# A second mixer's scan: weight subtractions on GpSimd, keys ahead of queries, interleaving copies ahead of weight copies

## The chip, the cores and the metric

One core of one Trainium2 chip runs the whole program in one launch. The metric is the device time of one execution in microseconds. The kernel before takes 1975.9 us (median of three runs, 1975.22 to 1977.95). All arithmetic is 32-bit. Engines are called by the names of the profile: PE (TensorE), PEld (its weight loads), DVE (VectorE), ACT (ScalarE), POOL (GpSimd), SP (SyncE, which issues most DMAs).

## The reference

Two layers. Each has a half-step SwiGLU FFN, a token mixer, and a second half-step FFN, for 256 latent tokens and 256 context tokens. The mixer projects its input, runs a gated linear recurrence in both directions for four heads, and in parallel a pooling mixer:

```python
proj = u @ w_in
q, zf, zb, i, g, pv, ga, gb = jnp.split(proj, IN_SPLITS, axis=-1)
o, s_f, s_b = hgrn2_bidir(q, i, zf, zb, lb_f, lb_b, s0_f, s0_b)
if not need_out:
    return None, s_f, s_b
on = o * lax.rsqrt(jnp.mean(o * o, axis=-1, keepdims=True) + EPS)
a = (on.reshape(...) * hg_norm_w * jax.nn.silu(g))
p = pool_mixer(pv, pool_w, pool_scale, on_grid)
merged = jax.nn.sigmoid(ga) * (a @ w_a) + jax.nn.sigmoid(gb) * (p @ w_b)
return merged @ w_out, s_f, s_b
```

The recurrence is S_t = diag(f_t) S_{t-1} + k_t v_t^T, o_t = S_t^T q_t. In the second (last) layer the context tokens yield only their final states: queries are needed for 256 tokens, keys and gates still for 512. So the first mixer works on 512 tokens, the second on 256 for all but keys, gates and values.

## The kernel before, in words

**Weights in two parts.** Weights arrive in units of 128 x 1024 numbers, in a ring of four slots. For each unit SP issues a DMA into `raw` as soon as the slot's last unit is multiplied (`s_used`); ACT copies it to `w_hi` in the rounded format (`split_next`, L712, signal `s_hi`); DVE writes the rest, raw minus `w_hi`, to `w_lo`, which lies in the memory of `raw` (`split_lo`, L980, signal `s_lo`); PE multiplies w_hi by u_hi, w_hi by u_lo, and w_lo by u_hi (L333, L334, L335). Both splits run three units (`AHEAD`) ahead of PE.

**The scan.** Each head's 256-token recurrence is a tree of doubling blocks in ten steps. Step 0 is the diagonal; steps 1 to 7 join blocks of 1, 2, ... 64 tokens; step 8 joins the two 128-token halves; step 9 applies the context's final states. Array `S` (two buffers, one for even and one for odd heads) has four parts: part 0 forward keys, 1 and 2 queries, 3 backward keys; `T` has the gates' products over blocks. For step k:

- DVE updates the keys and queries with the gates (`carry` in `prepare_step`, L1186): two instructions in the first mixer, four in the second (parts 0, 1, 2, 3 in this order). The last one signals `s_prep`.
- ACT interleaves the directions into `mixed` by two copies, keys first, queries second (`mix_directions`, L825), signal `s_mix`. This is done for steps 1 to 7.
- PE multiplies keys by queries (L496), signal `s_score`.
- DVE merges the scores into `A` under a mask (`merge`, L1232) and doubles the gate products (`double_totals`, L1207).

**Order.** Nothing schedules: each engine runs its own list in the order in which the code writes it, and waits at semaphores. A head is 12 pieces. In each piece PE does half a weight unit of projections for the next head (in the last head: of the gate and pooling projections) and then one scan step. In piece p, DVE waits for mixing copy p, prepares step p+1, in odd pieces subtracts the weight unit (`lo_next`), then merges step p and doubles. In piece p, ACT first copies the weight unit (odd pieces), then interleaves step p+1, then does the projections' activations. Small parts of the head before stand between: `head_diag`, `head_gate` and `head_lo` on DVE (L1215, L1220) and `head_hi` on ACT (L837).

**After the scan** of a mixer ACT and DVE copy the pooling projection to `pv` (L899, L1297), PE multiplies it by box matrices (L633), which POOL's DMAs (`mixer_tables`, L312) have brought to memory that the scan used. POOL does only DMA issues and a few memsets.

Of the kernel before, what the change touches and what calls it, by code (L numbers as in the profile page):

```python
# [29 lines left out]
F32 = mybir.dt.float32  # L30
# [8 lines left out]
ALL = 2 * TOK  # L39
# [4 lines left out]
NH = 4  # L44
# [57 lines left out]
def program(nc, resid_in, c_in, c_cols_in, cols_in, poolw_in, box_in, masks_in, ident_in, weights, adaw, out):  # L102
    with ExitStack() as stack:
# [118 lines left out]
        s_vout = sem("v_out")  # L222
        s_sga = sem("sig_a_out")
        s_prep = sem("operands_ready")
        s_mix = sem("directions_mixed")
# [64 lines left out]
        def _(pool):  # L290
# [27 lines left out]
            load(ahead, N_ADA - ahead)  # L318
            mixer_tables(1)

# [383 lines left out]
        def _(act):  # L704
# [112 lines left out]
            def mix_directions(n, step, nt):  # L817


                act.wait_ge(s_prep, NSTEP * n + step + 1)  # L820

                act.wait_ge(s_score, NSTEP * n + step - 1)
                hb = 1 << (step - 1)
                for m, (array, other) in enumerate(((0, 3), (1, 2))):
                    ins = act.activation(view(mixed, (step % 2 * 2 + m) * ALL, [2 * hb, nt // (2 * hb)], [hb, 2], [1, hb]),  # L825
                                         view(S[n % 2], array * ALL, [2 * hb, nt // (2 * hb)],
                                              [(other - array) * ALL + hb, 2], [1, hb]), ACT.Copy)
                ins.then_inc(s_mix, 1)
# [10 lines left out]
            def mixer(layer, n_norm):  # L839
# [18 lines left out]
                for head in range(NH):  # L858
                    n = layer * NH + head
                    par = head % 2  # L860
                    for piece in range(12):
                        j = piece // 2
                        if piece % 2:
                            split_next(base + j - (base + j) % 4, None, (base + j) % 4 + AHEAD)
                        if piece < NLEVEL:
                            mix_directions(n, piece + 1, nt)
                        if piece % 2:
# [100 lines left out]
        def _(dve):  # L968
# [200 lines left out]
            def prepare_step(n, step):  # L1169
# [21 lines left out]
                else:  # L1191
                    carry(0, 1, 0, ALL, 0)
                    carry(1, 1, 0, nt, 1)

                if nt == ALL:
                    ins = carry(2, 2, 1, ALL, 0)
                else:
                    carry(2, 1, 1, nt, 0)
                    ins = carry(3, 1, 1, ALL, 1)
                ins.then_inc(s_prep, 1)  # L1200
# [34 lines left out]
            def mixer(layer, n_norm):  # L1235
# [14 lines left out]
                for head in range(NH):  # L1250
                    n = n0 + head
                    par = head % 2
                    for piece in range(12):
                        j = piece // 2
                        lo_next = lambda: split_lo(base + j - (base + j) % 4, None, (base + j) % 4 + AHEAD)
                        if piece < NSTEP:
# [36 lines left out]
                    base += 6  # L1293

                dve.wait_ge(s_used, base)
                for t in range(nt // P // 2, nt // P):
# [229 lines left out]
```

## Time and profile before

| | |
|---|---|
| median of three runs | 1975.9 us |
| the profiled execution | 1976.28 us, span 1974.6 us |
| PE busy | 1942.9 us (98%) |
| DVE busy | 1262.6 us (64%) |
| ACT busy | 795.4 us (40%) |
| POOL busy | 72.7 us (4%) |
| granted TensorE clock | 0.997 of full speed |

The span runs from the first to the last instruction that the profiler sees; the execution's own time is 1.7 us more. The scan of the first mixer lies at about 459 to 643 us of the span, that of the second at about 1560 to 1688 us. Idle time is shown in front of an instruction with the engine whose work ended it.

### The profile page before, as it was taken

The page shows a single profiled execution, that of the slowest core. Times are in us where ns is not written, and L with a number is a line of the kernel's source. Part 1 is how long each engine was busy: PE and PEld are TensorE (multiplying, and loading weights), DVE is VectorE, ACT ScalarE, POOL GpSimd, SP SyncE. Part 2 cuts the span into 40 slices and gives each one's busy share as a digit, 9 for nine tenths or more (in the row PEclk, how much of TensorE's full clock was granted, in tenths as well). Part 3 has the DMA queues.
Part 4 walks back from the last instruction along what each step waited for, and adds up shares of the span by engine and source line. Part 5 has one row for each costly group of instructions (what it writes and reads, how often), then busy time and mean ns, then how long its engine had stood idle before and what let it go on. Part 6 is the DMA issues. An engine that isn't in the chain of part 4 may idle for free.

```text
span 1974.6 us, 29022 instructions
## 1 busy us (share of the span) xinstructions
PE 1942.9 (98%) x10024; PEld 1649.4 (84%) x10024; DVE 1262.6 (64%) x2048; ACT 795.4 (40%) x1083; POOL 72.7 (4%) x142
## 2 busy tenths in 40 slices
PE   7999999999999999999999999999999998999998
PEld 2888888888888888888888888888888897999998
DVE  3667576676665466667566675755757678575555
ACT  2422222345554323532222353223224576456444
POOL 0000000000000000000000000000100000000000
PEclk9999999999999999999999999999999999999999
DMA  7345445433223243345454534444544333545554
GB/s 311 107 150 190 139 162 177 158 105 111 71 69 112 87 139 121 111 139 202 138 160 168 161 96 151 169 160 141 205 140 129 99 105 105 178 149 182 183 184 154
DMA packets 78664, 287.39 MB, mean 146 GB/s; under 512 B 8768, under 2 KB 10048, under 8 KB 77824
## 3 DMA queue, kind: packets, MB, share of 16 engines
q1 hardware_dynamic: 58912, 212.89, 32.5%
q0 software_dynamic: 19392, 73.34, 11.4%
q8 instruction: 46, 0.75, 0.2%
q14 instruction: 26, 0.21, 0.0%
q10 hardware_dynamic: 288, 0.18, 0.0%
HBM read 285.34 MB, written 1.05 MB: 145 GB/s over the span
## 4 chain that ended last, share of the span: by engine, by line
PE 92%; DVE 3%; DMA 2%; issue 1%; ACT 1%; ACTq 0%; DVEq 0%; SPq 0%
PE bank L333 26%; PE bank L334 26%; PE bank L335 26%; DMA raw<-weights 2%; PE bank L689 1%; PE bank L496 1%; PE bank L556 1%; PE bank L550 1%; PE bank L551 1%; ACT w_hi L712 1%; DVE S L1186 1%; PE bank L633 1%; PE bank L361 1%; PE bank L417 1%; PE bank L411 0%
## 5 line engine op out<-in xcount | busy, mean ns | idle before, releaser
L333 PE MATMUL bank<-u_hi,w_hi 128*128 128x512 f32 (+1 forms) x1824 | 664.0, 364 | 0.4 <-DVE w_lo L980 0.4
L334 PE MATMUL bank<-u_lo,w_hi 128*128 128x512 f32 (+1 forms) x1824 | 654.7, 359 | 0.0
L335 PE MATMUL bank<-u_hi,w_lo 128*128 128x512 f32 (+1 forms) x1824 | 654.6, 359 | 0.0
L980 DVE TENSOR_TENSOR w_lo<-raw,w_hi 128x1024 fp32r<-128x1024 f32 x384 | 469.1, 1223 | 245.8 <-ACT w_hi L712 216.5
L712 ACT ACTIVATE w_hi<-raw 128x1024 fp32r<-128x1024 f32 x384 | 405.1, 1056 | 435.1 <-DMA raw<-weights 434.4
L333 PEld LDWEIGHTS bank<-u_hi,w_hi 128*128 128x128 f32 x1824 | 344.5, 189 | 51.5 <-DVE w_lo L980 1.0
L335 PEld LDWEIGHTS bank<-u_hi,w_lo 128*128 128x128 f32 x1824 | 344.3, 189 | 51.3
L334 PEld LDWEIGHTS bank<-u_lo,w_hi 128*128 128x128 f32 x1824 | 344.6, 189 | 50.3 <-issue 0.7
L333 PE MATMUL bank<-hid_hi,w_hi 128*128 128x512 f32 (+1 forms) x832 | 299.1, 360 | 0.7 <-DVE w_lo L980 0.5
L991 DVE SCALAR_TENSOR_TENSOR junk<-ada_raw,silu_c 128x1024 bf16<-128x1024 f32 x256 | 298.2, 1220 | 0.5 <-DVE junk L991 0.5
L335 PE MATMUL bank<-hid_hi,w_lo 128*128 128x512 f32 (+1 forms) x832 | 298.2, 358 | 0.0
L334 PE MATMUL bank<-hid_lo,w_hi 128*128 128x512 f32 (+1 forms) x832 | 298.2, 358 | 0.0
L778 ACT ACTIVATE silu_t<-bank 128x512 f32<-128x512 f32 (+1 forms) x88 | 47.9, 545 | 355.9 <-PE bank L335 353.5
L1107 DVE TENSOR_TENSOR hid_t<-silu_t,bank 128x512 f32<-128x512 f32 (+1 forms) x88 | 54.7, 621 | 206.3 <-ACT silu_t L778 205.9
L333 PEld LDWEIGHTS bank<-hid_hi,w_hi 128*128 128x128 f32 x832 | 157.1, 189 | 24.8 <-DVE w_lo L980 0.7
L335 PEld LDWEIGHTS bank<-hid_hi,w_lo 128*128 128x128 f32 x832 | 157.1, 189 | 23.2
L334 PEld LDWEIGHTS bank<-hid_lo,w_hi 128*128 128x128 f32 x832 | 157.2, 189 | 23.1 <-issue 0.2
L1082 DVE SCALAR_TENSOR_TENSOR h<-bank,gate_c,h 128x256 f32 (+1 forms) x192 | 85.3, 479 | 74.5 <-PE bank L335 72.0
L305 POOL DMA_DIRECT2D ada_raw<-adaw x126 | 66.8, 530 | 1209.1 <-DVE junk L991 1209.1
L1111 DVE TENSOR_TENSOR hid_lo<-hid_t,hid_hi 128x512 f32 (+1 forms) x88 | 55.1, 626 | 77.8 <-ACT hid_hi L780 77.8
L1186 DVE TENSOR_TENSOR S<-S,T 128x256 f32<-128x256 f32 (+1 forms) x192 | 78.7, 465 | 19.7 <-PE bank L487 11.6
L780 ACT ACTIVATE hid_hi<-hid_t 128x512 f32 (+1 forms) x88 | 51.0, 580 | 71.0 <-DVE hid_t L1107 71.0
(162 smaller groups left out, 1504.5 us busy)
## 6 DMA issues: line engine op xcount, KB each, us to landing
raw<-weights SPq DMA_DIRECT2D x384, 512.0 KB, 3.5
ada_raw<-adaw POOLq DMA_DIRECT2D x128, 512.0 KB, 4.3
start_w<-weights SPq DMA_DIRECT2D x8, 1024.0 KB, 12.5
box<-box POOLq DMA_DIRECT2D x4, 1024.0 KB, 8.0
h<-resid SPq DMA_DIRECT2D x1, 2048.0 KB, 19.5
silu_c<-c POOLq DMA_DIRECT2D x1, 1024.0 KB, 5.2
out<-sig_a SPq DMA_DIRECT2D x8, 128.0 KB, 2.0
poolw<-poolw POOLq DMA_DIRECT2D x2, 256.0 KB, 10.0
```

Of the source, the lines that this page charges most:

```text
L305: pool.dma_start(ada_raw[:, j, :], adaw[bass.ds(i * 2 + j, 1)].rearrange("a p n -> (a p) n")).then_inc(s_aland[j], 16)
L333: pe.matmul(ps, w_hi[:, slot, k, :], hi(k), start=first, stop=False)
L334: pe.matmul(ps, w_hi[:, slot, k, :], lo(k), start=False, stop=False)
L335: mm = pe.matmul(ps, w_lo[:, slot, k, :], hi(k), start=False, stop=last)
L712: act.activation(view(w_hi, (j % RING) * UNIT, [1, UNIT]), raw[:, j % RING, :], ACT.Copy).then_inc(s_hi, 1)
L780: act.activation(hid_hi[:, bass.ds(i * 2 + b, 1), 0:nt].rearrange("p a n -> p (a n)"), hid_t[:, b, 0:nt], ACT.Copy).then_inc(s_hid_hi, 1)
L980: dve.tensor_tensor(view(w_lo, (j % RING) * UNIT, [1, UNIT]), raw[:, j % RING, :], view(w_hi, (j % RING) * UNIT, [1, UNIT]).bitcast(F32), ...
L991: dve.scalar_tensor_tensor(out=junk[:, s, :], in0=ada_raw[:, j, :], scalar=1.0, in1=silu_c[:, s, :], op0=ALU.mult, op1=ALU.mult, accum_out ...
L1082: ins = dve.scalar_tensor_tensor(out=hd, in0=ps[:, span(s)], scalar=gate_c[:, s, bass.ds(d, 1)], in1=hd, op0=ALU.mult, op1=ALU.add)
L1107: dve.tensor_tensor(hid_t[:, b, 0:nt], silu_t[:, b, 0:nt], bank[2 * b + 1][:, 0:nt], ALU.mult).then_inc(s_up_free, 1)
L1111: dve.tensor_tensor(hid_lo[:, bass.ds(f, 1), 0:nt].rearrange("p a n -> p (a n)"), hid_t[:, b, 0:nt], hid_hi[:, bass.ds(f, 1), 0:nt].rearra ...
L1186: return dve.tensor_tensor(t, t, view(Th, d * ALL + (1 - side) * hb, *cut, [0, hb]), ALU.mult)
```

## The change

Three edits:

1. On ACT, in both mixers, the interleaving copies of a piece stand ahead of its weight copy.
2. In the second mixer, for steps 2 and up, DVE updates parts 3 and 0 (both keys) first and signals `s_keys`; the first interleaving copy waits for that alone, the second for `s_prep`.
3. The 24 weight subtractions of the second mixer's scan move from DVE to POOL. They stand behind all loads of the modulation weights; POOL's three table DMAs stand between the 22nd and the 23rd. DVE waits for the last of them before its `pv` copy.

```diff
             load(ahead, N_ADA - ahead)
-            mixer_tables(1)
+
+            scan_unit = mix_base(1) + 8 + AHEAD
+            pool.wait_ge(s_lo, scan_unit - START)
+            for u in range(scan_unit, scan_unit + 6 * NH):
+                if u == scan_unit + 6 * NH - 2:
+                    mixer_tables(1)
+                pool.wait_ge(s_hi, u + 1 - START)
+                pool.tensor_tensor(view(w_lo, u % RING * UNIT, [1, UNIT]), raw[:, u % RING, :],
+                                   view(w_hi, u % RING * UNIT, [1, UNIT]).bitcast(F32), ALU.subtract
+                                   ).then_inc(s_lo, 1)
...
             def mix_directions(n, step, nt):
-                act.wait_ge(s_prep, NSTEP * n + step + 1)
-
                 act.wait_ge(s_score, NSTEP * n + step - 1)
+                if nt < ALL and step > 1:
+                    act.wait_ge(s_keys, (NSTEP - 2) * (n - NH) + step - 1)
                 hb = 1 << (step - 1)
                 for m, (array, other) in enumerate(((0, 3), (1, 2))):
+                    if m or nt == ALL or step == 1:
+                        act.wait_ge(s_prep, NSTEP * n + step + 1)
...
+                        if piece < NLEVEL:
+                            mix_directions(n, piece + 1, nt)
                         if piece % 2:
                             split_next(base + j - (base + j) % 4, None, (base + j) % 4 + AHEAD)
-                        if piece < NLEVEL:
-                            mix_directions(n, piece + 1, nt)
...
                 else:
                     carry(0, 1, 0, ALL, 0)
-                    carry(1, 1, 0, nt, 1)
+                    carry(3, 1, 1, ALL, 1).then_inc(s_keys, 1)
...
                 else:
-                    carry(2, 1, 1, nt, 0)
-                    ins = carry(3, 1, 1, ALL, 1)
+                    carry(1, 1, 0, nt, 1)
+                    ins = carry(2, 1, 1, nt, 0)
                 ins.then_inc(s_prep, 1)
...
-                        lo_next = lambda: split_lo(base + j - (base + j) % 4, None, (base + j) % 4 + AHEAD)
+                        lo_next = lambda: None if layer else split_lo(
+                            base + j - (base + j) % 4, None, (base + j) % 4 + AHEAD)
...
+                if layer:
+                    dve.wait_ge(s_lo, base + AHEAD - START)
                 dve.wait_ge(s_used, base)
```

ACT, first mixer, second head, pieces 0 to 3, before (L825 interleaving copies, x2 is one step; L712 weight copy; L837 a part of the head before; the others are activations of projections):

```order
L832 ACTIVATE r_cols<-bank,eps_c 128x4
L825 ACTIVATE mixed<-S_67 128x512 x2
L712 ACTIVATE w_hi<-raw 128x1024
L825 ACTIVATE mixed<-S_67 128x512 x2
L809 ACT_TABLE_LOAD
L809 ACTIVATE S_63<-bank 128x512
L825 ACTIVATE mixed<-S_67 128x512 x2
L837 ACTIVATE hid_hi<-head_t 128x512
L712 ACTIVATE w_hi<-raw 128x1024
L825 ACTIVATE mixed<-S_67 128x512 x2
L813 ACT_TABLE_LOAD
```

The same place of the changed kernel (L837 is now the interleaving copy, L722 the weight copy, L849 the part of the head before):

```order
L844 ACTIVATE r_cols<-bank,eps_c 128x4
L837 ACTIVATE mixed<-S_67 128x512 x4
L722 ACTIVATE w_hi<-raw 128x1024
L819 ACT_TABLE_LOAD
L819 ACTIVATE S_63<-bank 128x512
L837 ACTIVATE mixed<-S_67 128x512 x2
L849 ACTIVATE hid_hi<-head_t 128x512
L837 ACTIVATE mixed<-S_67 128x512 x2
L722 ACTIVATE w_hi<-raw 128x1024
L823 ACT_TABLE_LOAD
```

Each weight copy of an odd piece has moved behind the interleaving copies of that piece. DVE's list in the first mixer has not moved: its subtraction still stands between the carries and the merge.

DVE, second mixer, third head, pieces 2 and 3, before (L1186 carries, in parts 0, 1, 2, 3; L980 subtraction; L1232 merge; L1207 doubling):

```order
L1232 COPY_PREDICATED A_65<-masks,bank 128x2x128
L1207 TENSOR_TENSOR T_64<-T_64 128x256
L1215 TENSOR_TENSOR head_t<-head_t,bank 128x256
L1186 TENSOR_TENSOR S_63<-S_63,T_64 128x64x4
L1186 TENSOR_TENSOR S_63<-S_63,T_64 128x32x4 x2
L1186 TENSOR_TENSOR S_63<-S_63,T_64 128x64x4
L980 TENSOR_TENSOR w_lo<-raw,w_hi 128x1024
L1232 COPY_PREDICATED A_65<-masks,bank 128x2x128
L1207 TENSOR_TENSOR T_64<-T_64 128x128
L1220 TENSOR_TENSOR hid_lo<-head_t,hid_hi 128x256
```

The same pieces of the same head in the changed kernel:

```order
L1244 COPY_PREDICATED A_65<-masks,bank 128x2x128
L1219 TENSOR_TENSOR T_64<-T_64 128x256
L1227 TENSOR_TENSOR head_t<-head_t,bank 128x256
L1198 TENSOR_TENSOR S_63<-S_63,T_64 128x64x4 x2
L1198 TENSOR_TENSOR S_63<-S_63,T_64 128x32x4 x2
L1244 COPY_PREDICATED A_65<-masks,bank 128x2x128
L1219 TENSOR_TENSOR T_64<-T_64 128x128
L1232 TENSOR_TENSOR hid_lo<-head_t,hid_hi 128x256
```

The subtraction is gone from DVE's list, and the two keys' carries (the longer shape, 512 tokens) stand ahead of the two queries' carries.

POOL, end of its list, changed kernel (L306 the last loads of modulation weights, L327 subtractions, L313 and L314 the tables' DMAs):

```order
L306 DMA ada_raw<-adaw 128x1024
L302 REGISTER_ALU
L302 COMPARE_AND_BRANCH
L327 ISA
L327 TENSOR_TENSOR w_lo<-raw,w_hi 128x1024 x22
L313 DMA box_60<-box 128x2048
L313 DMA box_61<-box 128x2048
L314 DMA poolw<-poolw 128x512
L327 TENSOR_TENSOR w_lo<-raw,w_hi 128x1024 x2
```

Before, the tables' DMAs came directly behind the loads; now 22 subtractions stand ahead of them and two behind.

## Rows read from the trace of the kernel before

**Rows 1.** The page: span, then busy time of each engine.
```profile
span 1974.6 us, 29022 instructions
PE 1942.9 (98%) x10024; PEld 1649.4 (84%) x10024; DVE 1262.6 (64%) x2048; ACT 795.4 (40%) x1083; POOL 72.7 (4%) x142
```

**Rows 2.** The page's chain of waits, shares of the span by engine.
```profile
PE 92%; DVE 3%; DMA 2%; issue 1%; ACT 1%; ACTq 0%; DVEq 0%; SPq 0%
```

**Rows 3.** Waits of PE, first mixer's scan (440 to 640 us); us, times, longest.
```profile
PE bank L496 <- ACT mixed L825: 0.5, 1, 0.5
```

**Rows 4.** Waits of PE, second mixer's scan (1500 to 1695 us).
```profile
PE bank L496 <- ACT mixed L825: 5.8, 5, 1.8
PE bank L478 <- DVE S L1186: 2.0, 2, 1.3
PE bank L633 <- DVE pv L1297: 1.1, 1, 1.1
```

**Rows 5.** Timeline, PE, first mixer: start, us, instruction, [idle before].
```profile
464.22 1.13 PE L496 MATMUL bank<-mixed 128*128 128x128 f32 x8 [0.53 <-ACT mixed L825]
471.56 1.05 PE L496 MATMUL bank<-mixed 128*128 128x128 f32 x8
...
522.16 1.05 PE L496 MATMUL bank<-mixed 128*128 128x128 f32 x8
525.78 1.05 PE L496 MATMUL bank<-mixed 128*128 128x128 f32 x8
```

**Rows 6.** Timeline, ACT, first mixer.
```profile
462.45 1.63 ACT L825 ACTIVATE mixed<-S 128x512 f32<-128x512 f32 x2 [3.81 <-DVE S L1176]
...
518.52 1.04 ACT L712 ACTIVATE w_hi<-raw 128x1024 fp32r<-128x1024 f32 x1
519.47 1.14 ACT L825 ACTIVATE mixed<-S 128x512 f32<-128x512 f32 x2
...
523.73 1.16 ACT L825 ACTIVATE mixed<-S 128x512 f32<-128x512 f32 x2 [0.72 <-DVE S L1186]
```

**Rows 7.** Timeline, DVE, first mixer, second head.
```profile
517.87 1.28 DVE L1186 TENSOR_TENSOR S<-S,T 128x512 f32<-128x512 f32 x2
519.60 1.23 DVE L980 TENSOR_TENSOR w_lo<-raw,w_hi 128x1024 fp32r<-128x1024 f32 x1 [0.44 <-ACT w_hi L712]
520.74 0.73 DVE L1232 COPY_PREDICATED A<-masks,bank 128x512 f32<-128x512 uint8 x1
521.36 0.41 DVE L1207 TENSOR_TENSOR T<-T 128x128 f32<-128x128 f32 x1
521.80 0.69 DVE L1220 TENSOR_TENSOR hid_lo<-head_t,hid_hi 128x512 fp32r<-128x512 f32 x1
```

**Rows 8.** Timeline, PE, second mixer.
```profile
1585.80 0.70 PE L478 MATMUL bank<-S 128*128 128x256 f32 x2 [0.72 <-DVE S L1186]
...
1665.27 0.68 PE L496 MATMUL bank<-mixed 128*128 128x128 f32 x4 [1.16 <-ACT mixed L825]
...
1671.47 0.68 PE L496 MATMUL bank<-mixed 128*128 128x128 f32 x4 [1.55 <-ACT mixed L825]
```

**Rows 9.** Groups of instructions, DVE, 1500 to 1695 us, shapes apart.
```profile
L980 DVE TENSOR_TENSOR w_lo<-raw,w_hi 128x1024 fp32r<-128x1024 f32 x38 | 46.4, 1223 | 36.5 <-ACT w_hi L712 28.0 <-PE bank L480 8.3
L1207 DVE TENSOR_TENSOR T<-T 128x512 f32<-128x512 f32 x4 | 2.7, 686 | 0.0
```

**Rows 10.** Groups of instructions, POOL, whole span, shapes apart.
```profile
L291 POOL MEMSET ones<- 128x128 f32 x1 | 0.2, 205 | 0.3 <-POOLq L1517 0.3
L292 POOL MEMSET eps_c<- 128x1 f32 x1 | 0.1, 99 | 0.0
```

**Rows 11.** Timeline, all engines, end of the second mixer's scan.
```profile
1677.32 1.05 POOL L312 DMA_DIRECT2D box<-box  x2 [183.90 <-PE bank L496]
...
1687.78 1.06 ACT L712 ACTIVATE w_hi<-raw 128x1024 fp32r<-128x1024 f32 x1 [1.95 <-DMA raw<-weights]
...
1691.24 1.10 PE L633 MATMUL bank<-box,pv 128*128 128x256 f32 x4 [1.14 <-DVE pv L1297]
```

More of the change, by code:

```diff
@@ L223, in program @@
         s_sga = sem("sig_a_out")
+        s_keys = sem("keys_ready")
         s_prep = sem("operands_ready")
```

## The prediction

> **What bounds the kernel now.** I read the page's totals first, then the chain of waits, then PE's waits in each mixer's scan, then the timelines of the places where something waits. PE is busy 98% of the span [rows 1] and makes 92% of the chain that ended last [rows 2]. So time can be won only where PE stands idle, and it is lost wherever some other engine becomes late for PE. In the first mixer's scan PE waits once for an interleaving copy, 0.5 us [rows 3]: nothing is to be won there. In the second it waits five times for interleaving copies, 5.8 us, twice for carries, 2.0 us, and once for the copy to pv, 1.1 us [rows 4]. There PE's work per piece is shorter (256 tokens), while DVE's is not: DVE ends last. The largest possible gain is therefore about 9 us, 0.45% of the time.
>
> **Edit 1 in the first mixer: the weight copy goes behind the interleaving copies.** ACT has room, but DVE is in order, and in this mixer it still subtracts the weight unit between its carries and its merge. Before, the weight copy ran during the carries, and DVE found it done or nearly done (idle 0.44 us in [rows 7]). Now the weight copy begins only when the interleaving copies end, and these begin only when the carries end. So DVE stands still for 1.15 + 1.05 us after the carries of every odd piece.
>
> Second head, from [rows 6, 7]. Carries start at 517.87 and end at 519.15 (unchanged, since they depend on PE's scores). Interleaving copies, 1.15: 520.35. Weight copy, 1.05: 521.4. Subtraction, 1.14 from its start to that of the merge: 522.6. Merge, 0.62: 523.2. Doubling and the part of the head before, 0.44 + 0.61: 524.25. Carries of step 5, 1.28: 525.55. Interleaving, 1.15: 526.7. PE starts about 0.15 later, at 526.85. Before, this copy ended at 523.73 + 1.16 = 524.89, and PE took it at 525.78 [rows 5]: 0.9 us of slack against 1.8 us of delay. PE waits 1.1 us.
>
> From there the chain closes on itself, from one odd step to the next: carries 1.28, interleaving 1.15, weight copy 1.05, subtraction 1.14, merge 0.62, doubling 0.3 (0.41 in [rows 7], and less in each step after), carries 1.28, interleaving 1.15, signals 0.2, together 8.2 us. PE's two pieces take 2 x 3.62 = 7.25 us [rows 5]. Step 7 waits another 0.9 us. So 2.0 us for the second head, and for the third, which repeats it. In the first head nothing of an earlier head stands between: from the end of the first copies (462.45 + 1.63 = 464.08, [rows 6]) the same chain with a longer doubling (0.69 for 512 wide, [rows 9]) ends at 472.7, PE wants it at 471.56 [rows 5]: 1.2 us, then 0.9 twice, 3.0 us. In the fourth head a projection's activation already delays PE a little; I take 1.7 us. Sum 8.7 us lost, in a scan that waited 0.5 us before. Bounds: 0 if the copies overlap in a way that I don't see, 11 us if every one of the twelve pairs costs 0.9.
>
> **Edits 1 and 2 in the second mixer.** Interleaving no longer stands behind a weight copy that itself waits for its DMA, and the keys' copy runs under the queries' carries, so one step's loop shortens by some 0.4 us. The 1.8 us wait of the first step [rows 4] stays: ahead of that step stands the subtraction of the unit before the moved ones, which is still DVE's. With DVE free of the subtractions the four other waits for copies (5.8 - 1.8 = 4.0 us, two of them in [rows 8]) and the two for carries (2.0 us) can go; ACT's table loads in the last head leave some 0.5. That is -5.5 us, if POOL's work costs DVE nothing.
>
> **Edit 3: the price of POOL's subtraction.** The trace has no two-input instruction on POOL. Its 128-wide memset takes 205 ns and its 1-wide one 99 ns [rows 10], so 0.83 ns per element and pass, 0.85 us for 1024. From below, DVE's own 1.22 us [rows 9]; from above, two reads and a write one after the other, 2.65 us. I take two passes, 1.8 us. For PE alone either is hidden: units are prepared three ahead, over 10 us.
>
> What is not hidden is DVE. The trace shows no moment in which POOL computes beside DVE, so its effect is bounded by two cases: none, or the two engines take turns at the memory for each instruction in which DVE reads two operands from it. These are the carries and doublings, which make up most of the chain. If they take turns, each subtraction that starts holds up the next doubling for 1.8 us, where before it took 1.14 us of DVE's time. At the 0.72 us wait in [rows 8] DVE's run was subtraction, merge, doubling, carries. The merge reads its scores from PSUM and may run beside the hold (0.3 us, half of the 0.62 for twice the tokens), so the run ends 1.8 - 1.14 - 0.3 = 0.4 us later, and where the hold of the odd piece before has pushed on this one as well, 1.0 us. That gives +1.0, +1.1, +0.4 us for three heads. In the fourth the shorter loop and the longer hold cancel. So +2.5 us instead of -5.5; up to +8 if the hold is 2.65 us and breaks in between the carries. I take turn-taking as the likelier: it is my choice, and no row decides it.
>
> The Trainium skill bears on this. "SBUF — State Buffer", section "Who interferes with whom", says that a VectorE instruction with two SBUF inputs contends with a GpSimd one that reads SBUF, and that the later one is blocked until the first ends. No run here shows it yet. "GPSIMD Engine Reference", section "Performance versus the Vector engine", has 4497 ns for a 2048-wide fp32 add against 2293 ns on VectorE; half of it, an estimate, is 2.2 us, and by that the sum would be some 2 us more. DVE's 1.22 us in this trace agrees with half of the page's VectorE figure.
>
> **The end of the scan.** POOL's list now has 22 subtractions ahead of the tables' DMAs. Before, they were issued at 1677.32 as soon as step 7 was scored; now the subtraction of that piece comes first, some 1.8 us. Behind, the last of the 24 weight units waited for its DMA until 1687.78, in competition with these tables; it is then subtracted, DVE copies pv, and PE starts at 1691.24 after 1.14 us idle [rows 11]. Now: later tables end later and hold the weight unit some 0.7 us longer; POOL's subtraction takes 0.7 us more than DVE's; and DVE's copy waits for it. +1.4 us (0.3 to 3).
>
> **The sum.** Against the profiled execution, 1976.28 us: +8.7 + 2.5 + 1.4 = +12.6, 1988.9 us. The median of the runs shown lies 0.4 lower: 1988.5 us.
>
> **Rivals.**
> - *POOL computes beside DVE freely.* +8.7 - 5.5 + 1.4 = +4.6, 1980.5 us. For it: nothing in the trace, as nothing against it.
> - *The first mixer absorbs the new order, engines take turns.* 0 + 2.5 + 1.4: 1979.8 us. For it: PE waits 0.5 us in that whole scan [rows 3]. Against: the slack before step 5 is 0.9 us and I count 1.8.
> - *Faster: the first mixer absorbs the order and POOL runs freely.* The second mixer's loop becomes shorter than PE's piece, its waits vanish: -5.5 + 1.4 = -4.1, 1971.8 us. It decides once DVE's delay per odd piece in the first mixer is under 0.9 us and a doubling beside a POOL subtraction keeps its length.
>
> **Chances.** Forecast 0.5; free POOL 0.25; first mixer absorbs, turns 0.15; faster 0.1. What a measurement of this kernel tells from no change is 0.2%, 4 us. The forecast and nearly all of the second case are slower; the third is about half within; of the last, two thirds faster. Faster 0.08, same 0.17, slower 0.75. Range 1976 to 1994: it leaves out the fastest case and holds of more than 2.65 us.
>
> **What would show it.** In the first mixer: DVE's subtraction idle some 2 us before it, behind the weight copy, in odd pieces; PE waiting for L496 two or three times a head, 7 to 10 us in all. If PE's waits there stay under 2 us, the first step is wrong. In the second: doublings or carries of two or more us beside a POOL subtraction, and PE waits of 8 to 13 us against 7.8; if doublings keep 0.2 to 0.7 us and the waits fall to 2 us, the free case holds. At the end: PE's idle before the first box product at 2 to 3 us instead of 1.14.

## The result and the profile after

The changed kernel takes 2006.9 us (median of four runs, 2002.81 to 2011.03) against 1976.9 us for the kernel before on the same chip: ratio 1.0151, interval 1.0138 to 1.0164. It is slower, as forecast, but by 30 us where 12.6 were forecast, and outside the range. Its profiled execution took 2002.81 us. Ratios compare a kernel with the kernel before on the same chip, whose median was 1976.2 us beside e1 to e4, 1978.4 beside e5 to e8 and 1977.6 beside e9 to e12. Executions of one kernel differ in their granted clock: the other three of the changed kernel took 4 to 8 us longer than the profiled one, at a mean of 0.990 to 0.991 against 0.993, and one of the ten of e6 took 3397.5 us at 0.649 and is left out of its ratio.

The page of the changed kernel: span and busy time, to be held against [rows 1].

```profile
span 2001.1 us, 29026 instructions
PE 1951.4 (98%) x10024; PEld 1654.2 (83%) x10024; DVE 1272.2 (64%) x2024; ACT 796.0 (40%) x1083; POOL 131.0 (7%) x166
```

Two things don't fit. DVE lost 24 instructions of 1.22 us, 29 us of work, and is 10 us busier. And PE is 8.5 us busier with the same 10024 matmuls. The first is a cost on DVE that the instruction list doesn't show; the second must be matmuls that took longer, at a slower clock or otherwise.

Below are the waits of PE in the first mixer's scan (440 to 660 us), and below them in the second's (1500 to 1725 us); us in total, times, longest. They answer to [rows 3, 4]. PE never waits for POOL's result itself in these scans: every wait is for a copy of ACT or a result of DVE.

```profile
PE bank L506 <- ACT mixed L837: 7.1, 9, 1.2
PE bank L560 <- ACT sig_a L888: 0.9, 1, 0.9
...
PE bank L506 <- ACT mixed L837: 9.0, 8, 2.3
PE bank L497 <- DVE S L1198: 5.6, 3, 2.2
PE bank L643 <- DVE pv L1312: 2.9, 1, 2.9
PE bank L488 <- DVE S L1198: 2.8, 1, 2.8
```

**First mixer.** The timeline of DVE in the second head answers to [rows 7]. The idle time before the subtraction was 0.44 us and is 2.2, behind ACT's weight copy (L722), which stands behind the interleaving copies.

```profile
521.22 1.29 DVE L1198 TENSOR_TENSOR S<-S,T 128x512 f32<-128x512 f32 x2
524.74 1.23 DVE L992 TENSOR_TENSOR w_lo<-raw,w_hi 128x1024 fp32r<-128x1024 f32 x1 [2.23 <-ACT w_hi L722]
525.88 0.73 DVE L1244 COPY_PREDICATED A<-masks,bank 128x512 f32<-128x512 uint8 x1
```

**Second mixer.** First POOL, then DVE, in the same stretch of the timeline.

```profile
1588.53 2.52 POOL L327 TENSOR_TENSOR w_lo<-raw,w_hi 128x1024 fp32r<-128x1024 f32 x1 [3.35 <-ACT w_hi L722]
1592.68 2.48 POOL L327 TENSOR_TENSOR w_lo<-raw,w_hi 128x1024 fp32r<-128x1024 f32 x1 [1.63 <-ACT w_hi L722]
1595.81 2.38 POOL L327 TENSOR_TENSOR w_lo<-raw,w_hi 128x1024 fp32r<-128x1024 f32 x1 [0.65 <-ACT w_hi L722]
```

```profile
1588.73 2.47 DVE L1198 TENSOR_TENSOR S<-S,T 128x128 f32<-128x128 f32 x1
1591.13 0.43 DVE L1244 COPY_PREDICATED A<-masks,bank 128x256 f32<-128x256 uint8 x1
1591.46 0.18 DVE L1219 TENSOR_TENSOR T<-T 128x16 f32<-128x16 f32 x1
1591.74 1.16 DVE L1198 TENSOR_TENSOR S<-S,T 128x256 f32<-128x256 f32 x4
1592.83 0.45 DVE L1244 COPY_PREDICATED A<-masks,bank 128x256 f32<-128x256 uint8 x1
1593.16 2.04 DVE L1219 TENSOR_TENSOR T<-T 128x8 f32<-128x8 f32 x1
1595.23 3.31 DVE L1198 TENSOR_TENSOR S<-S,T 128x256 f32<-128x256 f32 x4
```

Read the ends together. POOL's subtraction of 1588.53 ends at 1591.05, and the small carry that came 0.2 us after it ends at 1591.20: 2.47 us for one that took 0.29 before. The doubling at 1593.16 writes 8 columns and takes 2.04 us; it ends at 1595.20, POOL's subtraction of 1592.68 at 1595.16. The run of four carries takes 1.16 us nearly alone and 3.31 with a subtraction in its midst. The merge at 1592.83, whose scores come from PSUM, runs inside a subtraction and keeps its 0.45 us. PE waits 2.80 us for those carries, until 1598.59. In the whole scan 19 of POOL's 24 subtractions catch an instruction of DVE in this way: 13 carries, three doublings and three products of the first step (L1187). Each of them takes 1.75 to 2.58 us and ends 0.03 to 0.28 us after POOL's.

Groups of DVE, shapes apart (busy, mean ns | idle before): the carries before (1500 to 1695 us), then carries and merges of the changed kernel and POOL's group (1500 to 1725 us). The merges took 443 ns before.

```profile
L1186 DVE TENSOR_TENSOR S<-S,T 128x256 f32<-128x256 f32 x64 | 27.0, 422 | 4.1 <-ACT mixed L825 3.4
L1186 DVE TENSOR_TENSOR S<-S,T 128x128 f32<-128x128 f32 x64 | 15.6, 286 | 0.0
```

```profile
L1198 DVE TENSOR_TENSOR S<-S,T 128x128 f32<-128x128 f32 x64 | 39.6, 659 | 0.0
L1198 DVE TENSOR_TENSOR S<-S,T 128x256 f32<-128x256 f32 x64 | 28.6, 488 | 3.7 <-PE bank L497 1.5 <-ACT mixed L837 1.4
L1244 DVE COPY_PREDICATED A<-masks,bank 128x256 f32<-128x256 uint8 x28 | 12.4, 442 | 1.8 <-PE bank L506 1.5
...
L327 POOL TENSOR_TENSOR w_lo<-raw,w_hi 128x1024 fp32r<-128x1024 f32 x24 | 58.7, 2446 | 151.7 <-ACT w_hi L722 151.7
```

**The clock.** Windows of 2 us at the end of the scan: after busy times (PE, PEld, DVE, ACT, POOL) stand the granted clock (1.00 is 2.4 GHz, 0.50 is 1.2), the DMA share and GB/s. The row behind them is PE's box products there, and the last one the same products before.

```profile
1712.00:1714.00 2.00, 0.56 (x5) 0.35 (x3) 0.00 (x0) 1.97 (x4) 1.73 (x1) 1.00 0.31 74
1714.00:1716.00 2.00, 0.51 (x2) 0.49 (x3) 1.31 (x4) 1.98 (x3) 0.62 (x1) 1.00 0.67 238
1716.00:1718.00 2.00, 2.00 (x8) 1.59 (x7) 1.14 (x2) 1.99 (x4) 0.00 (x0) 0.64 0.01 4
1718.00:1720.00 2.00, 2.00 (x6) 1.64 (x5) 1.10 (x1) 0.56 (x3) 0.00 (x0) 0.50 0.00 0
```

```profile
1715.49 5.38 PE L643 MATMUL bank<-box,pv 128*128 128x256 f32 x16 [2.94 <-DVE pv L1312]
```

```profile
1691.24 3.69 PE L633 MATMUL bank<-box,pv 128*128 128x256 f32 x16 [1.14 <-DVE pv L1297]
```

After 2.94 us without work PE soon runs at half its clock, and the 16 box products take 5.38 us where the same 16 took 3.69. That comes on top of the wait. Two more such stretches lie in this stage, behind waits of 2.23 us (until 1630.9) and 2.28 us (until 1692.2). But not every wait of this length is followed by one. Behind the longest wait for carries, 2.80 us, the clock stays at 1.00, and so it does behind one of 2.24 us (until 1666.6):

```profile
1598.59 0.70 PE L488 MATMUL bank<-S 128*128 128x256 f32 x2 [2.80 <-DVE S L1198]
```

```profile
1600.00:1602.00 2.00, 2.00 (x16) 1.95 (x15) 1.37 (x4) 0.60 (x1) 0.00 (x0) 1.00 0.00 0
```

**The account.** Two stages are taken between the three places where DVE prepares a norm (`diag`): ahead of the first mixer (411.5 us before, 411.3 after), ahead of the second, and ahead of the last FFN. So differences elsewhere fall out. The first time in each row is the norm ahead of the second mixer, in the next row that ahead of the last FFN. Kernel before, then changed kernel:

```profile
L1023 DVE TENSOR_TENSOR diag<-ident,r_cols x2: 424/425/426, 1518.2 to 1518.8; 128x256 f32<-128x256 f32 x2
L1023 DVE TENSOR_TENSOR diag<-ident,r_cols x2: 424/424/425, 1768.8 to 1967.1; 128x256 f32<-128x256 f32 x2
```

```profile
L1035 DVE TENSOR_TENSOR diag<-ident,r_cols x2: 425/426/426, 1527.4 to 1528.0; 128x256 f32<-128x256 f32 x2
L1035 DVE TENSOR_TENSOR diag<-ident,r_cols x2: 424/424/424, 1794.7 to 1993.6; 128x256 f32<-128x256 f32 x2
```

The stage with the first mixer is 9.4 us longer (1116.1 against 1106.7), that with the second 16.7 us (267.3 against 250.6), the rest 0.4: together the 26.5 us between the spans. Below is the same reading of e1 to e10, as differences from before, each from one profiled execution. PE's waits are those of the second mixer's scan up to the box products (8.9 us before); "clock" is the time that the lowered clock takes from the second stage, summed over windows of 2 us as (1 - granted clock) x 2:

| kernel | first stage | second stage | PE's waits, second scan | clock |
|---|---|---|---|---|
| changed kernel | +9.4 | +16.7 | +11.4 | 5.1 |
| e1, first mixer's order back | +0.1 | +15.9 | +10.8 | 5.1 |
| e2, order alone | +8.1 | +17.9 | +10.7 | 6.8 |
| e3, POOL alone | +0.1 | +17.8 | +10.6 | 6.8 |
| e4, keys alone | 0.0 | -0.5 | -1.8 | 1.7 |
| e5, POOL subtracts for nobody | 0.0 | +46.0 | +33.9 | 10.3 |
| e6, POOL fills for nobody | 0.0 | -1.2 | -1.0 | 0 |
| e7, subtraction in quarters | +9.4 | +4.5 | +3.2 | 0 |
| e8, DVE subtracts late | +0.1 | +3.7 | +0.5 | 3.4 |
| e9, the same, old order | 0.0 | -0.1 | -1.8 | 1.9 |
| e10, quarters, first mixer's order back | 0.0 | +6.3 | +3.6 | 1.7 |

Waits and clock make up the second stage in every row to within about 2 us.

### The profile page after: what moved, and what is told of

The parts are those of the page before. It is cut to its first block, busy times and chain, and to the rows that moved or that the text cites. A ratio compares the mean times of both kernels' runs of the same rounds, so it can differ in the third digit from the quotient of the medians.

```text
span 2001.1 us, 29026 instructions
## 1 busy us (share of the span) xinstructions
PE 1951.4 (98%) x10024; PEld 1654.2 (83%) x10024; DVE 1272.2 (64%) x2024; ACT 796.0 (40%) x1083; POOL 131.0 (7%) x166
## 4 chain that ended last, share of the span: by engine, by line
PE 89%; DVE 5%; issue 2%; ACT 2%; DMA 1%; POOLq 0%; POOL 0%; ACTq 0%; DVEq 0%; SPq 0%
PE bank L343 25%; PE bank L344 25%; PE bank L345 25%; DVE S L1198 2%; PE bank L699 1%; ACT mixed L837 1%; PE bank L506 1%; PE bank L560 1%; PE bank L561 1%; PE bank L566 1%; DMA raw<-weights 1%; ACT w_hi L722 1%; DVE T L1219 1%; PE bank L371 1%; PE bank L643 1%
## 5 line engine op out<-in xcount | busy, mean ns | idle before, releaser
L992 DVE TENSOR_TENSOR w_lo<-raw,w_hi 128x1024 fp32r<-128x1024 f32 x360 | 439.6, 1222 | 248.7 <-ACT w_hi L722 227.8
L722 ACT ACTIVATE w_hi<-raw 128x1024 fp32r<-128x1024 f32 x384 | 404.6, 1055 | 429.6 <-DMA raw<-weights 428.6
L306 POOL DMA_DIRECT2D ada_raw<-adaw x126 | 66.5, 528 | 1210.6 <-DVE junk L1003 1210.6
L1198 DVE TENSOR_TENSOR S<-S,T 128x256 f32<-128x256 f32 (+1 forms) x192 | 106.9, 612 | 18.3 <-PE bank L497 8.8
L837 ACT ACTIVATE mixed<-S 128x512 f32<-128x512 f32 (+1 forms) x112 | 57.4, 551 | 74.4 <-DVE S L1198 57.0
```

The lines of the kernel that those rows point to most:

```text
L306: pool.dma_start(ada_raw[:, j, :], adaw[bass.ds(i * 2 + j, 1)].rearrange("a p n -> (a p) n")).then_inc(s_aland[j], 16)
L722: act.activation(view(w_hi, (j % RING) * UNIT, [1, UNIT]), raw[:, j % RING, :], ACT.Copy).then_inc(s_hi, 1)
L992: dve.tensor_tensor(view(w_lo, (j % RING) * UNIT, [1, UNIT]), raw[:, j % RING, :], view(w_hi, (j % RING) * UNIT, [1, UNIT]).bitcast(F32), ...
L1198: return dve.tensor_tensor(t, t, view(Th, d * ALL + (1 - side) * hb, *cut, [0, hb]), ALU.mult)
```

## The experiments

The theory after the result: POOL and DVE take turns, for the whole of an instruction, wherever both read two operands from SBUF; the order costs the first mixer what was forecast; the rest is clock. The rivals: POOL's result comes too late for PE; any work of POOL slows DVE; the clock fell for another reason.

**e1: the old order back in the first mixer.**

```diff
+                        if piece % 2 and not layer:
+                            split_next(...)
                         if piece < NLEVEL:
                             mix_directions(n, piece + 1, nt)
-                        if piece % 2:
+                        if piece % 2 and layer:
                             split_next(...)
```

> The changed kernel with ACT's old order in the first mixer only (weight copy ahead of the interleaving copies). Theory: the new order costs the first mixer its 17 or so waits of DVE for the weight copy and through them PE's 8.0 us of waits (7.1 for interleaving copies and 0.9 for a projection's activation); they go back to 0.7 us, and nothing else moves: 2006.9 - 7.5 = 1999 us (1996 to 2002). Rival (what the first mixer loses would be lost later anyway, at the next point where PE waits): 2004 to 2007 us.

Measured: 1993.75 us, ratio 1.0097 (1.0079 to 1.0115). The first stage is back (+0.1), PE waits there 0.6 + 0.2 us, and the second stays at +15.9. So edit 1 costs the first mixer 9.3 us, and the two mixers' losses add up. The time lies below the expected 1996 to 2002 us: the two profiled spans differ by 9.9 us, the medians by 13, and no trace shows the rest.

**e2: edit 1 alone**, in both mixers, on the kernel before.

```diff
-                        if piece % 2:
-                            split_next(...)
                         if piece < NLEVEL:
                             mix_directions(n, piece + 1, nt)
+                        if piece % 2:
+                            split_next(...)
```

> The kernel before with edit 1 alone: interleaving copies ahead of weight copies in both mixers, DVE subtracts everywhere. Theory (a subtraction in DVE's list must not stand behind a weight copy that stands behind copies that need DVE's own carries): first mixer +7.5 us as in the changed kernel; second mixer a chain of 1.2 + 0.7 + 1.05 + 1.14 + 0.33 + 0.3 + 1.2 + 0.7 + 0.2 = 6.8 us for two pieces of which PE needs 3.75 (256 tokens) or 6.4 us (512): +8 to +15 us there, and some us of lower clock: 1993 to 2006 us. Rival (in the second mixer the copies won't wait behind the weights' DMAs any more, so that this edit alone gains there): 1976 + 7.5 - 4 = 1980 us.

Measured: 2002.33 us, ratio 1.0131 (1.0116 to 1.0145). The first mixer loses 8.1 us. The second loses 17.9, though POOL does nothing: the same mechanism as in the first, for DVE still subtracts here. Timeline of DVE there, and PE's waits in that scan (5.8 us before):

```profile
1626.42 1.23 DVE L980 TENSOR_TENSOR w_lo<-raw,w_hi 128x1024 fp32r<-128x1024 f32 x1 [1.74 <-ACT w_hi L712]
1627.57 0.43 DVE L1232 COPY_PREDICATED A<-masks,bank 128x256 f32<-128x256 uint8 x1
```

```profile
PE bank L496 <- ACT mixed L825: 18.2, 10, 3.1
```

**e3: edit 3 alone** (POOL's subtractions; ACT and the carries as before).

```diff
+                pool.wait_ge(s_hi, u + 1 - START)
+                pool.tensor_tensor(view(w_lo, ...), raw[:, u % RING, :], view(w_hi, ...), ALU.subtract).then_inc(s_lo, 1)
...
-                        lo_next = lambda: split_lo(...)
+                        lo_next = lambda: None if layer else split_lo(...)
```

> The kernel before with edit 3 alone: the 24 subtractions on GpSimd, everything else as before. Theory (each GpSimd subtraction blocks VectorE's two-operand instructions for its 2.4 us): carries or doublings of 2 to 3 us beside each, PE's waits in the second mixer's scan about 20 us against 8.9, first mixer unchanged, some us of lower clock: 1987 to 1997 us. Rival (the engines work side by side and only the later copy to pv costs): 1976 - 5 + 3 = 1974 us.

Measured: 1997.13 us, ratio 1.0114 (1.0092 to 1.0136), at the upper edge of what was expected. First stage +0.1, second +17.8. With 24 instructions of 1.22 us taken off DVE, PE waits 10.6 us longer (19.5 us, about 20 expected).

**e4: edit 2 alone** (keys ahead of queries).

```diff
-                    carry(1, 1, 0, nt, 1)
+                    carry(3, 1, 1, ALL, 1).then_inc(s_keys, 1)
...
-                    carry(2, 1, 1, nt, 0)
-                    ins = carry(3, 1, 1, ALL, 1)
+                    carry(1, 1, 0, nt, 1)
+                    ins = carry(2, 1, 1, nt, 0)
```

> The kernel before with edit 2 alone: keys' carries first with their own signal, the first interleaving copy waits for that alone. Theory: the copies end some 0.35 us earlier in each step of the second mixer where ACT is free; PE's waits there fall from 8.9 to 6 to 8 us: 1974 to 1976.5 us, at most 0.1% faster. Rival (the copies wait for the weight copy and its DMA, not for the carries): the same time as before within 0.5 us.

Measured: 1977.47 us, ratio 1.0005 (0.9995 to 1.0015): no change, and not the gain of up to 0.1% that was expected. PE's waits fall from 8.9 to 7.1 us, as expected, but this profile has one low stretch of the clock (1568 to 1573 us) that the profile before has not.

**e5: the kernel before, with POOL subtracting for nobody.** DVE keeps its own subtractions.

```diff
+                pool.wait_ge(s_hi, u + 1 - START)
+                pool.tensor_tensor(ada_raw[:, 1, :], ada_raw[:, 0, :], silu_c[:, 0, :], ALU.subtract).then_inc(s_side, 1)
```

> The kernel before, DVE subtracting as there, with 24 GpSimd subtractions added in the second mixer's scan whose operands (the table ada_raw and silu_c) and result nobody uses, each released by the same count of ScalarE's weight copies as in the changed kernel. If DVE and GpSimd take turns wherever both read SBUF with two operands, DVE's carries, doublings and its own weight subtractions there are held up to 2.4 us each as in the changed kernel, PE waits 15 to 22 us in this scan where it waited 8.9, and the time is 1990 to 2005 us, worse than with the subtraction moved since DVE keeps its 24 x 1.22 us. Rival: what was late in the changed kernel was the subtraction's place (a result that comes late from GpSimd), not the sharing: then work for nobody costs nothing, 1975 to 1979 us, and the carries keep their 286 and 422 ns.

Measured: 2021.38 us, ratio 1.0214 (1.0196 to 1.0232), above the expected 1990 to 2005; PE waits 42.8 us in this scan where 15 to 22 were expected. No operand or result of these instructions concerns anyone, so a loss of this kind needs no late result. Below are groups of DVE and POOL, 1500 to 1725 us. DVE's own subtraction is held now (1223 ns before), and so are some of its doublings (that of 8 columns took 0.17 us), and POOL is held too (2848 ns against 2446). The carries, which I expected to be held, take 421 and 320 ns in the mean, hardly more than before. So it is not always the same instruction that is caught.

```profile
L989 DVE TENSOR_TENSOR w_lo<-raw,w_hi 128x1024 fp32r<-128x1024 f32 x37 | 64.9, 1757 | 27.9 <-ACT w_hi L721 19.5 <-PE bank L489 8.4
...
L1216 DVE TENSOR_TENSOR T<-T 128x8 f32<-128x8 f32 x4 | 6.8, 1689 | 0.0
...
L328 POOL TENSOR_TENSOR ada_raw<-ada_raw,silu_c 128x1024 f32<-128x1024 f32 x23 | 65.5, 2848 | 162.4 <-ACT w_hi L721 162.4
```

**e6: the same places, POOL only writes.**

```diff
+                pool.memset(ada_raw[:].rearrange("p a n -> p (a n)"), 0.0)
+                pool.memset(silu_c[:, 0, :], 0.0).then_inc(s_side, 1)
```

> As the run with subtractions for nobody, but GpSimd only writes: fills of 128x2048 and 128x1024 fp32 in the same places (some 3 us in all a time, more than the 2.4 us of a subtraction, with no read). If the turn-taking comes from reading operands, DVE's carries keep 286 and 422 ns and the time is 1975 to 1979 us. Rival: any work of GpSimd on SBUF holds DVE's two-operand instructions, then the carries go to 500 to 700 ns in the mean and the time is 1990 us or more.

Measured: 1978.36 us, ratio 0.9994 (0.9983 to 1.0005). POOL is busy 66.5 us in this scan, more than in the changed kernel, and DVE's carries keep their length within 1 ns (422 and 286 before):

```profile
L1196 DVE TENSOR_TENSOR S<-S,T 128x256 f32<-128x256 f32 x64 | 27.0, 421 | 4.0 <-ACT mixed L835 3.3
L1196 DVE TENSOR_TENSOR S<-S,T 128x128 f32<-128x128 f32 x64 | 15.6, 285 | 0.0
...
L328 POOL MEMSET ada_raw<- 128x2048 f32 x24 | 43.6, 1816 | 130.6 <-ACT w_hi L722 130.6
```

So it is the reading that collides. The Trainium skill, "SBUF — State Buffer", section "Who interferes with whom", says just this: a VectorE instruction with two SBUF inputs contends with a GpSimd instruction that reads SBUF, not with one that only writes it, and the later one is blocked for the whole of the other. These traces agree: the fills left the carries alone, and the subtractions of 2.45 us held DVE up to their end.

**e7: the changed kernel, each subtraction of POOL in four quarters.**

```diff
+                for q in range(4):
+                    at_q = u % RING * UNIT + q * 256
+                    ins = pool.tensor_tensor(view(w_lo, at_q, [1, 256]), raw[:, u % RING, q * 256:(q + 1) * 256], ...)
+                ins.then_inc(s_lo, 1)
```

> The changed kernel with each of GpSimd's 24 subtractions (128x1024, 2446 ns) cut into four of 128x256, back to back. If DVE is held until the instruction of GpSimd that runs beside it has ended, the longest hold falls from some 2.4 us to some 0.65 us, the L1198 carries of 128x128 fall from 659 ns to 350 to 450 ns, and the time is 1990 to 2000 us, above the 1976 before since the first mixer's wait of 7 us stays. Rival: four instructions in a row are handed the memory without a gap for DVE; then each hold stays at 2.4 to 2.8 us and the time stays at 2003 to 2012 us.

Measured: 1992.83 us, ratio 1.0074 (1.0057 to 1.009). The second stage falls from +16.7 to +4.5 us, with the same work on the same engines. PE's waits there are 12.1 us instead of 20.3, the longest 1.8, and the clock stays at 1.00 throughout the stage. DVE and POOL alternate: a quarter takes 0.81 us, and no held carry or doubling is longer than 0.96 us, where the longest was 2.58. The late result is excluded here once more: a unit's four quarters together take longer than the one subtraction did, and PE waits less.

```profile
1578.97 2.26 DVE L1200 TENSOR_TENSOR S<-S,T 128x256 f32<-128x256 f32 x4
1581.16 0.44 DVE L1246 COPY_PREDICATED A<-masks,bank 128x256 f32<-128x256 uint8 x1
...
L1200 DVE TENSOR_TENSOR S<-S,T 128x128 f32<-128x128 f32 x64 | 31.1, 525 | 0.0
...
L329 POOL TENSOR_TENSOR w_lo<-raw,w_hi 128x256 fp32r<-128x256 f32 x96 | 75.1, 813 | 124.7 <-ACT w_hi L724 124.7
```

The run of carries shown takes 2.26 us, but another at 1691.06 us takes 3.24, nearly the 3.31 of above. The small carries came out at 525 ns where I expected 350 to 450, and all carries together are busy 64.4 us, against 68.2 in the changed kernel and 42.6 before: the sum of the holds hardly shrinks, the longest one does.

**e8: nothing on POOL; edits 1 (second mixer) and 2, and DVE subtracts behind merge and doubling there.**

```diff
-                            if piece % 2:
+                            if piece % 2 and not (layer and piece <= NLEVEL):
                                 lo_next()
...
                                 double_totals(n, piece + 1)
+                            if layer and piece % 2 and piece <= NLEVEL:
+                                lo_next()
```

> Nothing on GpSimd: keys ahead of queries, ScalarE's interleaving copy ahead of the weight copy in the second mixer alone, and there DVE's weight subtraction of an odd piece put behind that piece's merge and doubling, so that it no longer waits in front of them for ScalarE's late weight copy. In the run with the new order alone PE waited 18.2 us for the interleaving copies of this scan, since the subtraction stood idle for ScalarE ahead of the merge. If that was the cause, PE waits 4 to 8 us here (8.9 before), and the time is 1971 to 1977 us. Rival: the later subtraction (1.22 us) now stands in front of the next piece's carries, and PE waits as long as before or longer for the operands: 1977 to 1990 us.

Measured: 1979.48 us, ratio 1.001 (0.9998 to 1.0022): no gain, outside the expected 1971 to 1977 and within the rival's range. The waits fall from e2's 19.6 us to 9.4, where edit 2 alone is worth 1.8 (e4): the subtraction that stands waiting for the late weight copy was e2's cause in this mixer. But 9.4 is 0.5 more than before, and the stage is 3.7 us longer. Two low stretches of the clock, 3.4 us together, make up the rest.

**e9: edit 2 and the late subtraction, ACT's old order.**

> Keys ahead of queries, and in the second mixer DVE's subtraction of an odd piece behind that piece's merge and doubling; ScalarE keeps the order of before, GpSimd does nothing. With ScalarE's new order in the second mixer too, PE waited 9.4 us in that scan, as long as before (9.4), and two waits of 2.1 and 2.7 us were each followed by a stretch at a granted clock of 0.5. If it is ScalarE's order that made those, PE waits 6 to 8 us here and the time is 1972 to 1976 us. Rival: the later subtraction itself delays the next piece's carries; then 1977 to 1982 us.

Measured: 1976.02 us, ratio 0.9995 (0.9985 to 1.0004): no gain that can be measured. The waits are 7.1 us, as in e4. Of e8's two long waits the one for a copy is gone, so it came with ACT's order; the other, ahead of the box products, is still 2.0 us (2.7 in e8) and still comes with a low stretch, so it did not.

**e10: e7 with e1's edit**, a test of whether the causes add up.

> The changed kernel with GpSimd's subtraction in four quarters and ScalarE's order of before in the first mixer. The causes should add up: the first mixer goes back to its time before (its stage was 9.4 us longer in the changed kernel and 0.1 us with the order back), the second keeps the 4.5 us of the run in quarters. The time is then 1979 to 1984 us, that is 3 to 6 us above before. Rival: the quarters only looked cheap since the late first mixer had shifted the transfers; then 1985 to 1994 us.

Measured: 1983.07 us, ratio 1.0027 (1.0016 to 1.0038), inside the expected 1979 to 1984. They do: the first stage is as before, and the second is at +6.3 us against e7's +4.5, with one low stretch (1.7 us) that e7 has not.

**e11 and e12: two waits put into the kernel before**, each for two fills on POOL; PE idle in them (e11), or first multiplying for nobody (e12). This is the second wait; the first stands ahead of the box products in the same form, with `bank[4]`.

```diff
+                    for _ in range(28):        # e12 only
+                        pe.matmul(bank[1][:, 0:nt], u_hi[:, 0, 0:P], u_hi[:, 1, 0:nt], start=True, stop=True)
+                    pe.wait_ge(s_gap, 2)
```

> The kernel before; in the second mixer PE waits twice for a pair of GpSimd fills (some 3.6 us): ahead of the box products and ahead of the last products of the branches. PE is idle in these waits. If an idle TensorE is followed by a stretch at a granted clock of 0.5, the profile shows such a stretch behind each, and the time is 7.2 us of waiting less what was waited there anyway (1 to 2 us), and 1.5 to 2 us for each stretch: 1984 to 1988 us. Rival: the low stretches of the changed kernel do not come from the idle time; then the clock stays at 1.00 and the time is 1981 to 1984 us.

> The same two waits as in the run with the idle gaps, but PE first multiplies 28 times for nobody (256 columns each, some 3.4 us) into a free bank, and then waits for the same fills, so that only some tenths of idle time are left. If the clock falls behind idle time, it stays at 1.00 here and the time is 3 to 4 us below that of the idle gaps, 1981 to 1984 us. Rival: the fall has another cause (the place, the fills); then both take the same time.

Measured: 1987.92 us (ratio 1.0052, 1.0038 to 1.0065) idle and 1984.01 us (1.0037, 1.0023 to 1.005) filled. The intervals overlap, so the times alone don't decide; the clock does. The same windows at the second wait, e11 (PE idle until 1709.27) and then e12:

```profile
1706.00:1708.00 2.00, 0.00 (x0) 0.00 (x0) 0.85 (x2) 1.06 (x1) 1.94 (x2) 0.95 0.00 0
1710.00:1712.00 2.00, 2.00 (x12) 2.00 (x11) 0.00 (x0) 0.00 (x0) 0.00 (x0) 0.50 0.00 0
1712.00:1714.00 2.00, 2.00 (x11) 2.00 (x11) 0.00 (x0) 0.00 (x0) 0.00 (x0) 0.50 0.03 8
```

```profile
1706.00:1708.00 2.00, 2.00 (x19) 2.00 (x18) 0.86 (x2) 1.50 (x2) 1.94 (x2) 1.00 0.16 66
1710.00:1712.00 2.00, 2.00 (x17) 2.00 (x18) 0.00 (x0) 0.00 (x0) 0.00 (x0) 1.00 0.00 0
1712.00:1714.00 2.00, 2.00 (x19) 2.00 (x18) 0.81 (x3) 0.00 (x0) 0.00 (x0) 1.00 0.00 0
```

At this place it is the idle time that brings the clock down: filled, it stays up. At the first place it fell in both profiles. In e12 PE had been idle for 1.79 us ahead of the 28 products there; these then took 5.07 us, against 3.69 at the second place. Whether those 1.79 us were the cause isn't shown. The mean clock of all five executions points the same way: 0.993 to 0.994 in e11, and 0.994, 0.995 and three times 0.997 in e12, where 0.997 is that of the profile before, which has no low stretch in this scan. So e12 shows one half of what I expected of it.

## Why the prediction was right in sign and short by more than half

For the second stage the sum had +2.5 for the holds, +1.4 for the end of the scan and nothing for the clock, +3.9 in all. The profiled executions show +9.6 us of waits in the scan, +1.8 at its end and 5.1 of clock, and the stage is 16.7 us longer.

- **Edit 1 in the first mixer: right.** Forecast +8.7. Measured +9.4 in the stage, +8.1 with the edit alone, 9.3 regained by undoing it; PE waits for L506 nine times, 7.1 us, within the 7 to 10 named. The idle time of some 2 us before DVE's subtraction is there, 2.23. Of the 9.4 us the waits make 7.3; for the other 2.1 I have no row, the clock stood at 1.00.
- **Taking turns: the choice was right, its size was not.** This is the step that failed. I sized a hold at 1.8 us, from two passes of a memset [rows 10], and it is 2.45; its own upper bound, 2.65, was nearer. So was the estimate of 2.2 us from the Trainium skill's "GPSIMD Engine Reference", section "Performance versus the Vector engine", which I had set beside the sum. I then let it meet only the doubling, and only where PE had waited before, +2.5 us, so 10.3 us of waits in the scan proper with the 7.8 of before. They were 17.4. Of the 19 instructions held only three are doublings and 13 are carries, and they stand anywhere in the chain; e3 shows 10.6 us more of waits, end of the scan included, without edits 1 and 2. My bound of +8 with "a hold of 2.65 us that breaks in between the carries" was the right picture, and the 9.6 us more of waits lie even above it.
- **The low clock: left out.** 5.1 of the 16.7 us in the second stage are no waits but matmuls at 1.2 GHz behind some of them. One more low stretch lies just behind the stage, but costs little there: from the norm to the end it is 206.4 us against 205.8. The first box products of before, 1.10 us for four [rows 11], were in my hands, and nothing in the sum asked at what clock they would run after a longer idle time. The medians are 30 us apart and the profiled spans 26.5; most of the difference lies in the executions with the lower mean clock, of which there is no trace.
- **Edits 1 and 2 freed of DVE's work, -5.5 us: not tested.** No run takes the subtractions off DVE without giving POOL work that holds it. Edit 2 alone lowers PE's waits by 1.8 us and the time not at all (e4, e9). Edit 1 in this mixer only fails to harm if DVE's subtraction is out of its way (e2 against e8).
- **The end of the scan: right in path, its size partly luck.** Forecast +1.4, and PE's wait before the box products went from 1.1 to 2.9 us, +1.8, in the 2 to 3 us named. The path is the one named: DVE's copy to pv stands idle for 5.8 us behind POOL's last subtraction, which waited for ACT's copy and this for its DMA. But the wait varies with what comes before: with the same POOL list it was 0.9 us in e1 and 2.3 in e3, and without any subtraction on POOL 2.7 in e8 and 2.0 in e9.
- **Rivals.** POOL freely beside DVE fell with the rows and with e5. "The first mixer absorbs the order" fell with the nine waits; so did the faster case, which needed both.

Open: what brings the clock down after one wait and not after another. In e7 and in the kernel before, a wait of 1.8 us passed without a fall; in e4 one of 1.8 us was followed by one. The wait of 2.80 us at 1598.59 passed without it in the changed kernel, and the same wait of 2.80 us in e1, whose second mixer is the same, was followed by one (0.72 in the window of 1590 to 1592 us, then 0.50). So the length of a wait alone does not decide. A low stretch also stands at the norm ahead of the last FFN in the changed kernel (1794 to 1799 us) and in e1, e8, e9, e11 and e12, and not before, where PE's waits are as short as in the others (at most 0.7 us each).

## What to carry to other kernels

Work moved from VectorE to GpSimd is not gone from VectorE if both read two operands from SBUF: count each instruction on GpSimd as a hold of up to its full length that can hit any instruction of VectorE on the critical chain that reads two operands from SBUF, and if it must be there, cut it short (e7: 12 us back for the same work, 5 of them clock). In an in-order list, moving a step back on one engine moves everything that waits for it on the others; look for what is queued behind that waiter. And where PE's waits grow, their price can be more than their length: in the changed kernel's second scan three of the five waits of over 2 us were followed by a low stretch that cost 1.7 us.

## What the runs showed of the hardware that I had not expected

- GpSimd's subtraction of 128x1024 takes 2446 ns, twice VectorE's 1223; cut in four, 813 ns a quarter in company.
- A doubling of 8 columns took 2.04 us and a carry of 128x128 2.47 us beside it, while fills of 1816 ns on GpSimd changed the carries by at most 1 ns in the mean.
- A fall to the clock of 0.50 took 1.7 us in e4, e9 and e10, which have one each in the second stage, and 3.4 in e8, which has two. Behind the 4.1 us of idle time in e11 the clock was low for some 7 us, part of it while PE stood still.
